# Down projection of a gated FFN in seven block products instead of eight, in five stages instead of three

## What is computed

```python
def conv_ffn(hn, w_ffn_in, conv_w, conv_b, w_ffn_down):
    dt = hn.dtype
    u, v = jnp.split(hn @ w_ffn_in, 2, axis=-1)
    pad = CONV_W // 2
    up = jnp.pad(u, ((0, 0), (pad, pad), (0, 0)))
    L = u.shape[1]
    uc = conv_b
    for t in range(CONV_W):
        uc = uc + up[:, t:t + L] * conv_w[t]
    return (jax.nn.gelu(uc) * v).astype(dt) @ w_ffn_down
...
        h = h + conv_ffn(rmsnorm(h, norm_ffn[l]), w_ffn_in[l], conv_w[l], conv_b[l],
                         w_ffn_down[l])
    return rmsnorm(h, norm_final)
```

## Time and profile before

| | us |
|---|---|
| median of 3 runs | 1263.61 |
| the profiled execution | 1264.54 |
| its span | 1262.7 |
| FFN from the last long stop of PE to the end (769.58 to 1262.70) | 493.1 |
| of it: up projection | 305.4 |
| down chunks 1 and 2 | 66.1 each |
| last chunk with the end | 55.5 |

### The profile page before, as it was taken

The page is one execution under the profiler, slowest core; times in us unless marked ns, Lnnn a source line. Parts: engine busy times, 40 slices in busy tenths (PEclk is TensorE's granted clock), DMA queues, the critical chain, the costliest instruction groups (busy, mean ns, idle before and its releaser), DMA issues.

```text
span 1262.7 us, 18036 instructions
## 1 busy us (share of the span) xinstructions
PE 1232.3 (98%) x7088; PEld 1120.7 (89%) x7088; DVE 711.9 (56%) x969; ACT 490.9 (39%) x724; POOL 128.9 (10%) x93
## 2 busy tenths in 40 slices
PE   6999999999999999999999988999999999999998
PEld 5999899989998998888888878998889998899986
DVE  7494586377368463223223698775237774337755
ACT  5353344245146152212221255554125653135534
POOL 0000000000000000000000303430124420124200
PEclk9999999999999999999999999999999999999999
DMA  4311111101121112121215102222201213112122
GB/s 171 136 35 51 63 51 51 62 33 50 34 78 36 46 37 68 67 67 50 76 56 184 34 34 86 82 68 78 89 34 67 67 42 121 72 34 81 53 84 100
DMA packets 23180, 86.10 MB, mean 68 GB/s; under 512 B 2512, under 2 KB 2768, under 8 KB 23120
## 3 DMA queue, kind: packets, MB, share of 16 engines
q1 hardware_dynamic: 22544, 83.90, 19.4%
q10 hardware_dynamic: 576, 1.38, 0.3%
HBM read 82.12 MB, written 3.15 MB: 68 GB/s over the span
## 4 chain that ended last, share of the span: by engine, by line
PE 92%; DVE 4%; DMA 1%; issue 1%; ACT 1%; DVEq 1%; SPq 0%; ACTq 0%
PE ps L1425 58%; PE ps L1669 23%; PE ps L1522 3%; PE ps L1462 3%; PE ps L1515 1%; PE ps L1532 1%; PE ps L1450 1%; DVE af L1196 1%; PE ps L1452 1%; DVE h L1137 1%; DMA raw<-in_units 1%; DVE ring L1150 1%; PE ps L1407 0%; PE ps L1498 0%; PE ps L1507 0%
## 5 line engine op out<-in xcount | busy, mean ns | idle before, releaser
L1425 PE MATMUL ps<-hn,ring 128*128 128x256 f32 (+1 forms) x2544 | 462.5, 337 | 0.3 <-DVE hn L839 0.3
L1425 PEld LDWEIGHTS ps<-hn,ring 128*128 128x128 f32 x2544 | 388.3, 191 | 46.7 <-issue 0.7
L1669 PE MATMUL ps<-af,ring 128*128 128x384 f32 x1848 | 325.7, 336 | 10.9 <-DVE af L1196 3.9
L1669 PEld LDWEIGHTS ps<-af,ring 128*128 128x128 f32 x1848 | 321.3, 189 | 15.0 <-DVE af L1196 4.8
L1425 PE MATMUL ps<-ring,g 128*128 128x512 f32 x792 | 180.9, 390 | 0.8 <-issue 0.8
L1425 PEld LDWEIGHTS ps<-ring,g 128*128 128x128 f32 x792 | 148.4, 188 | 32.6 <-issue 2.0
L810 DVE TENSOR_TENSOR ring<-raw,ring 128x1024 fp32r<-128x1024 f32 x68 | 83.1, 1224 | 119.2 <-ACT ring L415 114.8
L464 ACT ACTIVATE sig<-ps 128x768 f32<-128x768 f32 x36 | 29.2, 812 | 179.9 <-PE ps L1425 179.8
L1150 DVE TENSOR_TENSOR ring<-raw,ring 128x512 fp32r<-128x512 f32 x88 | 74.0, 877 | 15.9 <-ACT ring L652 15.7
L415 ACT ACTIVATE ring<-raw 128x1024 fp32r<-128x1024 f32 x68 | 71.7, 1055 | 28.8 <-PE ps L1425 10.2
L1384 POOL TENSOR_TENSOR sums<-raw 128x512 f32<-128x512 f32 x1 | 1.3, 1289 | 706.9 <-DMA raw<-in_pairs 706.9
(11 more groups left out here) (158 smaller groups left out, 1210.5 us busy)
## 6 DMA issues: line engine op xcount, KB each, us to landing
raw<-in_units SPq DMA_DIRECT2D x90, 512.0 KB, 3.5
raw<-in_pairs SPq DMA_DIRECT2D x44, 512.0 KB, 3.4
strips<-in_strips SPq DMA_DIRECT2D x4, 896.0 KB, 4.5
x_in<-in_x_s SPq DMA_DIRECT2D x4, 512.0 KB, 5.5
h<-in_x_s SPq DMA_DIRECT2D x1, 2048.0 KB, 8.4
y_s<-hw SPq DMA_DIRECT2D x4, 512.0 KB, 2.6
x_in<-in_x_p SPq DMA_DIRECT2D x2, 512.0 KB, 7.5
h<-in_x_p SPq DMA_DIRECT2D x1, 1024.0 KB, 10.5
```

The costliest lines, as they stand in the source:

```text
L1425: ins = pe.matmul(out, w if stationary_w else x, x if stationary_w else w, start=start and i == 0, stop=stop and i == 2)
L1669: ins = pe.matmul(ps[:, bank, 0:HALF], ring[:, p, a, k * P:(k + 1) * P], af[:, x, b, k, :], start=first and k == 0 and j == 0, stop=k == H ...
```

## The change

w_ffn_down is made in seven block products too. A down pair q is gate tiles 2q and 2q+1 (11 pairs) by both halves of the output. The 2x2 blocks are: the tokens in two halves of 384 by the two gate tiles, and the two gate tiles by the two halves of the output. One product of a pair is 3 token tiles by 3 passes = 9 matmuls of 512 columns, so a pair is 63 matmuls (before: 2 gate tiles by 6 token tiles by 2 halves by 3 passes = 72).

- Stages: up pairs 0 to 4, then down pairs 0 and 1; 5 to 8, then 2 and 3; 9 to 12, then 4 and 5; 13 to 16, then 6 and 7; 17 to 21, then 8, 9 and 10. So all but the last stage take gate tiles that were made at least one up pair ago.
- Weight side: down pairs are loaded into the same two raw buffers in turn with the up pairs. They get the same four differences on POOL and 7 pieces of 512 columns through the ring. The difference S1 is now made in place over A11, so it waits until A11 is split. Pair 10 has a third buffer over `af`.
- Gate side: `gate` of an even tile writes `ge`. `gate` of an odd tile writes `cb` and makes four sums (S3, S2, S1, S4) of 384 columns. Seven forms are split into `gf`: one behind the even tile and six behind the odd tile. Before, one 768-column split followed each tile.
- Results: each of the 7 products of a stage ends in 3 residual sums of 128x512 on DVE (21 per stage, 105 in all; before 36). The next but one product writes the same banks and waits for them.
- End: the last product (A22) is made token tile by token tile for tiles 3 to 5, 9 matmuls each; tiles 0 to 2 are finished behind the product S4. Before, all six were finished one by one, behind 18 matmuls each.

The core of the diff:

```diff
-CHUNKS = ((0, 8), (8, 16), (16, 22))
+STAGES = ((0, 5, (0, 1)), (5, 9, (2, 3)), (9, 13, (4, 5)), (13, 17, (6, 7)), (17, 22, (8, 9, 10)))
+DOWN = [(A11, A12, S2, S1, S3, S4, A22)] * 4 + [(A11, A12, S2, S1, S4, S3, A22)]
+DEST = {A11: (0, 0), A12: (0, 0), S2: (0, 1), S1: (1, 1), S3: (1, 1), S4: (0, 1), A22: (1, 0)}
+ON_A = (A11, S2, S3, A22)
+        def difference(eng, j, x):
+            if x == S1:
+                eng.wait_ge(pu_ld[raw_of(j)], 16 * loads_of(j))
+                eng.wait_ge(pv_ld[raw_of(j)], 16 * loads_of(j))
+                eng.wait_ge(flo, ORD[j, A11] + 1)
+                ins = eng.tensor_tensor(b11, b12, b11, ALU.subtract)
+            elif x == S2:
...
+                ins = eng.tensor_tensor(second, b22, b11, ALU.subtract)
+        def down_bank(hi, x, t):
+            return 2 + t if x in ON_A else (5, BANK_A[hi % 2], 1)[t]
...
+            for j in SEQ:
+                b, prior = raw_of(j), prior_of(j)
...
                     sp.wait_ge(flo, ORD[prior, A22] + 1)
+                sp.dma_start(raws[b][:, 0, :], pairs[j, 0]).then_inc(pu_ld[b], 16)
                 if prior is not None:
                     sp.wait_ge(flo, ORD[prior, S4] + 1)
+                sp.dma_start(raws[b][:, 1, :], pairs[j, 1]).then_inc(pv_ld[b], 16)
...
             def gate(i):
+                q = i // 2
...
+                if i % 2 == 0:
+                    dve.tensor_tensor(ge[:], cb[:], v2[:], ALU.mult).then_inc(g32_done, 1)
+                    return
                 dve.tensor_tensor(cb[:], cb[:], v2[:], ALU.mult).then_inc(g32_done, 1)
+                dve.tensor_tensor(GATE[S3], ge[:, 0:HALF], ge[:, HALF:T], ALU.subtract).then_inc(gs_done, 1)
+                dve.tensor_tensor(GATE[S2], GATE[A22], GATE[S3], ALU.subtract).then_inc(gs_done, 1)
+                dve.tensor_tensor(GATE[S1], ge[:, HALF:T], GATE[A22], ALU.add).then_inc(gs_done, 1)
+                if i == NF - 1:
+                    gate_lo(i - 1)
+                dve.tensor_tensor(GATE[S4], GATE[A12], GATE[S2], ALU.subtract).then_inc(gs_done, 1)
...
+                for n, x in enumerate(DOWN[d]):
+                    if hi < NF or n < 6:
+                        lo_upto(PLACE[down_pair(qs[-1]), x] + 5)
+                    if hi < NF:
+                        down_sums(d, hi, qs, x, range(3))
+                        if n == 0:
+                            gate(hi - 1)
+                        elif n == 1:
+                            gate_lo(hi - 1)
+                        continue
...
+                    elif x == S3:
+                        dve.drain()
+                        for t in range(3, NT):
+                            dve.tensor_tensor(hw[:, t, early(t)], h[:, t, early(t)], wfin[:, early(t)], ALU.mult).then_inc(weighed, 1)
...
+            def down(hi, qs, d):
+                for n, x in enumerate(order):
+                    last = d == len(STAGES) - 1 and n == 6
+                    steps = [(q, t) for t in range(3) for q in qs] if last else [(q, t) for q in qs for t in range(3)]
+                    for q, t in steps:
                         if t == 0:
+                            pe.wait_ge(flo, ORD[down_pair(q), x] + 1)
+                            pe.wait_ge(g_lo, gate_form(q, x))
+                        if q == q0:
...
+                            elif x in (S2, S1, S3, S4, A22):
+                                before = {S2: A11, S1: A12, S3: S2, S4: S1, A22: S3}[x]
+                                pe.wait_ge(h_up, base + 3 * order.index(before) + t + 1)
```

More of the change, by code:

```diff
@@ new lines, in _ @@
+            base, order = down_base(len(STAGES) - 1), DOWN[-1]
+            for t in range(3):
+                act.wait_ge(h_up, base + 3 * order.index(S4) + t + 1)
+                squares(t, late(t), stat[:, 0, t:t + 1]).then_inc(sq_done, 1)
+            act.wait_ge(var_done, 2 * NT + 1)
+            act.activation(stat[:, 2, 0:3], stat[:, 1, 0:3], ACT.Sqrt).then_inc(sd_done, 1)
+            act.wait_ge(root_done, 1)
+            act.wait_ge(weighed, 3)
+            for t in range(3):
+                act.activation(hw[:, t, early(t)], hw[:, t, early(t)], ACT.Copy, scale=stat[:, 3, t:t + 1]).then_inc(out_rdy0, 1)
@@ L1309, in _ @@
                         join_third(i)
[L1310 to L1311 removed]
+                    if i > lo and i < NF - 1:
+                        gate_lo(i - 1)
                 lo_upto(PLACE[hi - 1, A22] + 5)
@@ L1329, in _ @@
-            dve.wait_ge(fin_ld, 16)
-            dve.wait_ge(fdone, len(ORD))
-            dve.drain()
-            for t in range(NT):
-                dve.tensor_tensor(hw[:, t, 0:PIECE], h[:, t, 0:PIECE], wfin[:, 0:PIECE], ALU.mult).then_inc(weighed, 1)
-            dve.wait_ge(half_sq, NT)
-            dve.tensor_scalar(stat[:, 5, :], stat[:, 4, :], 1.0 / D, EPS, ALU.mult, ALU.add).then_inc(half_var, 1)
-            for t in range(NT):
-                dve.wait_ge(dn, (2 * len(CHUNKS) - 1) * NT + t + 1)
-                residual(t, 1, t)
+                if hi == NF:
+                    gate(NF - 1)
+                    gate_lo(NF - 1)
@@ L1393, in _ @@
                 combine_tokens(pool, 0, x, s_done, 0)
-            combine(1, A22)
-            for i in range(2, NF):
-                for x in (S1, S3, S2, A22):
-                    combine(i, x)
+            pool.wait_ge(t_done, DIFF[1, S3])
+            for j, x in DIFFS[7:]:
+                difference(pool, j, x)
         @blk.tensor
@@ L1784, in _tables @@
+            for d, (lo, hi, qs) in enumerate(STAGES):
+                ffn(lo, hi, d)
+                down(hi, qs, d)
 def _tables():
@@ L1821, in _units @@
     out += [rows(w_out, k, half) for half in range(2) for k in range(KD // 2)]
-    for f0, f1 in CHUNKS:
-        out += [rows(w_ffn_down, k, half) for half in range(2) for k in range(f0 // 2, f1 // 2)]
     assert len(out) == UNITS
     pairs = [np.stack([cols(w_ffn_in, f * P), cols(w_ffn_in, FF + f * P)]) for f in range(NF)]
+    pairs += [np.stack([rows(w_ffn_down, q, 0), rows(w_ffn_down, q, 1)]) for q in range(NQ)]
     return np.stack(out), np.stack(pairs)
```

411 lines of the change are left out of this document (196 added, 215 removed).

## The result

The changed kernel takes 1284.28 us (median of 4 runs, 1282.7 to 1285.21), beside 1263.6 for the kernel before (4 runs, 1263.3 to 1263.95). The ratio is 1.0162, with a 95% interval of 1.0145 to 1.018. The profiled execution took 1282.7 us, its span is 1280.9. Forecast were 1253.2 us and a range of 1245 to 1264: the sign was wrong, and the time lies outside the range.

The account below looks back on a forecast made before the run. PE was taken as the bound, 98% busy, so time is matmuls times a rate. Up stages 307.0, down stages 118.9 and last stage 56.8 sum to 482.7 against 493.1: 10.4 us less, 1253.2 for the median, range 1245 to 1264.

Parts of the forecast that it names:

- five up stages: Up products of the FFN: 305.4 us before, plus 1.6 for stops at two more stage ends, so 307.0.
- four down stages: The first four down stages, two down pairs each: 29.7 us per stage including 1.0 loss, 118.9 in all.
- last stage and end: From the last down stage's start to the span's end: 55.9 us against 55.5 before, 56.8 with the clock.
- Matmuls: Down projection: 693 matmuls for 792, 99 fewer at 0.228 us each, 22.6 us less, all on PE's path.
- Down stages: DVE late through each down stage, S4's sums delaying the next up stage: 1.0 us loss each, ends 0 and 2.5.
- DVE in an up pair: DVE needs 10.8 us behind even tiles, 15.3 behind odd, mean 13.1 of PE's 14.6: hidden, nothing taken.
- sharp point: Next up pair's S1 needs `join_last` 10.4 us after S3 ended; ready at 8.8 to 10.2, so nothing taken.
- rival 3: Clock falls at each down stage's stop: four times 1.8 us, 1260.4; no change by this or half of rival 2: 0.10.
- Last stage: PE stands 2.7 us in the last down stage, waiting for the late gate tile's form for A11 of pair 10.
- The clock's 0.9: Lower clock behind the last stage's gate stop, 1.8 us in the earlier trace, may or may not follow: 0.9 taken.
- The end's count of DVE's instructions: DVE's work behind the last products: last stage and end 55.9 us against 55.5, so 6.2 of the gain lost.
- Rival 2: DVE bounds the down stages at S4's sums; all splits doubled, 5.6 us per stage, 1275.6. Slower: chance 0.15.

Follow-up runs that it names:

- experiment 1: Changed kernel with POOL's differences of the down pairs made over 8 of 512 columns, output not the reference's: 1249.67 us.
- experiment 2: Changed kernel with the four gate sums of each odd tile made over 8 of 384 columns, output not the reference's: 1271.42 us.
- experiment 3: Changed kernel with each 512-column POOL difference made as two instructions of 256 columns: 1285.3 us.
- experiment 4: Changed kernel with POOL holding a stage's down-pair differences until DVE made the third join of the last up pair: 1291.06 us.
- experiment 5: Changed kernel with the four gate sums of an odd tile behind the third join on DVE instead of ahead: 1285.95 us.
- experiment 6: Changed kernel; DVE makes down differences S1 and S2 (last stage: first pair only), POOL's S3 and A22 wait for residual sums; some DVE work reordered: 1262.98 us.
- experiment 7: As experiment 6, but DVE makes all eight down differences in each of the first four stages, POOL none: 1269.8 us.
- experiment 8: As experiment 6, with weight splits ahead of S3, S4, A22 reaching one piece less far, and DVE making all last-stage S1 and S2: 1253.71 us.
- experiment 9: As experiment 8, with last-stage A11 and A12 of pair 10 after those of pairs 8 and 9, weight splits two pieces less far there: 1249.45 us.

## Why the prediction was wrong, by its steps

Forecast were 482.7 us from the start of the FFN. Measured are 512.2, from 768.68 us on, 0.9 earlier than before: 29.5 more in the FFN, 28.6 more in the profiled time (1282.7 for 1254.1). By the terms:

| term | forecast | after | experiment 1 |
|---|---|---|---|
| five up stages | 307.0 | 335.8 | 308.9 |
| four down stages | 118.9 | 115.2 | 115.1 |
| last stage and end | 56.8 | 61.2 | 55.1 |
| sum | 482.7 | 512.2 | 479.1 |

(The down stages are 4 x 28.8, the last row is from the start of the last stage's first down matmul to the end of the span, and the up stages are the rest.)

- *Matmuls.* Right: 99 fewer, the rest at 0.228 us.
- *Down stages.* Forecast a loss of 1.0 each, came none. The splits average 0.84 to 0.86 us in them, within the 0.79 to 0.89 of the working, and a residual costs 0.63 instead of 0.68, 1.0 us less for the 21 of a stage. The differences of the next up pair start 22.2 us into the stage (947.27), where some 23 was forecast.
- *DVE in an up pair.* This step failed. It named the "sharp point" as `join_last` ahead of the next S1 and took nothing for it; for the last pair of a stage it said that the six splits of the odd tile end at -0.2 and that `join_third` is about 1.3 us late. Two things were wrong in it. First, it priced the odd tile's sums at 2.1 us and its product at the time alone, with POOL counted only in the mean of the weight splits (0.79), as if the differences stayed spread out. The row of 910.47 shows POOL released by one weight split, and from there nothing holds it: six differences run together, just where the sums are. Second, it had no line for who waits behind the sums. PE is ready for S4 2.9 us after S3 ended (0.58 and 2.35), and goes on 0.6 us behind the start of the third join (920.66, 921.25), so the join must start by 2.3. Without the burst it starts 1.3 after S3, as forecast (907.26 in experiment 1, where S3 ended at 905.95): a reserve of 1.0 us. The burst adds 9.84 - 3.56 = 6.3 us, 1.05 per difference, which is the reserve and the stop of 5.2. Four stops make 21.0 us.
- *The clock, rival 3.* Forecast for these stages: none. Behind the stop the 12 matmuls of the last product take 3.98 us, where half of the 24 in experiment 1 takes 2.23: 1.8 us each. (The four stages together last 375.7 us in after and 346.4 in experiment 1; less the stops of 21.0 that leaves 8.3, or 2.1 each.) The price of the rival (1.8 from the earlier trace rows) was right, its place not: the stop that does it is another one. Stops and clock together are 29.3 us. Less 2.4 in the last up stage, where experiment 1 stood 0.7 us longer and lost 1.6 to a lower clock (24 matmuls in 6.02 us for 4.43), and plus the 1.9 by which experiment 1 lies above 307.0, they are the 28.8 of the first row.
- *Last stage.* The gate's stop was forecast as 2.7 and is 2.83 in experiment 1, 6.82 in after, by the burst's 4.0 us on the convolution. The clock's 0.9 is 2.3 (35.10 for 32.8); in experiment 1 it is 0.1. The end's count of DVE's instructions holds: 55.1 against 55.9 without the clock term.
- *Rival 2* had the right resource ("now three differences run in a burst") and the wrong place and price. It priced DVE per weight split, doubled at most, at the S4 sums of the down stages. What decides is the number of POOL instructions that run while DVE has only instructions of that kind, each adding about 1.05 us, and it falls on the short sums as hard as on the long splits. The rival's worst case was 1275.6; the measured time lies above it.

The row that should have warned is the two splits of 2.38 us in the earlier trace rows: 0.5 us over their own 0.68 each, beside a single difference of 1.58. I read it as a ratio near 1.75 and averaged it over seven splits. Read as 1.0 us per difference, six differences add 6 us ahead of a join that has a reserve of about 1.0.

Some smaller figures of the working don't come out of its own terms, without changing its outcome. Of DVE's three waits in the earlier trace rows one (1.33) is for ACT, not for PE. The end loses 6.6 us of the gain, not 6.2 (55.9 against 55.5 less 27 x 0.228). With free stages and full clock the sum is 1248.2, not 1247.8. And the bounds of the terms give 1248.3 to 1264.1, not 1246 to 1261.

What stays open: why the down stages lost nothing was read from the means alone, the stops that the burst leaves behind the residuals in experiments 2 and 3 were not split into price and order, and no run looked at a down stage of three pairs with full clock ahead of it.

## What to carry to other kernels

Price contention per instruction of the other engine, not as a factor on your own: count how many of its instructions fall between two points that someone waits for, and multiply. Look for bursts: an engine whose inputs are all there works them off in a row when one release comes, and a mean taken over a stage hides it. If the colliding work must be done, put it beside instructions that don't collide (here the residuals), and hold it there by a wait, rather than shift the engine's own queue: experiments 4 and 5 only moved the stop, 6 to 9 removed it.

## What the runs showed of the hardware

**DVE and POOL take turns by whole instructions.** In the rows of after, POOL's first difference runs to 912.05. The product (0.95 us in experiment 1) started at 910.82, is recorded with 2.05 and ends at 912.87: 0.95 behind 911.9, so it began about when POOL ended. POOL's next starts at 912.13 and lasts 1.86, which is the 1.29 of experiment 6 plus 0.57, about to where the product ends (spans on POOL are rough; DVE's carry the argument). So an instruction's recorded time is its wait and its own time:

| DVE instruction, two operands in SBUF | alone | beside a 512-column difference |
|---|---|---|
| 8 columns | 0.16 | 1.23, 1.15 |
| 384 columns | 0.55 | 1.47 to 1.62 |
| 512 columns | 0.68 | 1.75 |
| 768 columns | 0.95 | 2.05 |
| 384 columns, difference of 256 | 0.55 | 1.09 |
| residual of 512, one operand in PSUM (mean of three in a row) | 0.63 | 0.63 |

The added time is 0.9 to 1.1 us in the first four rows, whatever the instruction's size. The turns are not strict: in experiment 5 POOL's first difference is recorded with 3.04 us from 911.76, while DVE's product (0.95) and split (0.69) beside it keep their own times, so there POOL waited for more than one instruction of DVE. The Trainium skill states this kind of rule (SBUF — State Buffer, section "SBUF: two separate sides"): the port pair that the two engines share is an exclusive lock that a VectorE instruction with two SBUF inputs, or the GpSimd instruction, holds for its whole length, while the other blocks. The recorded times agree, the untouched residual among them. In this kernel the price is what is left of a running difference, 0.9 to 1.1 us.

**A stop's length alone doesn't tell whether the clock falls.** Busy time by stretch in after (us, PE, PEld, DVE, ACT, POOL; then the granted clock):
```profile
826.15:829.80 3.65, 3.65 (x13) 3.65 (x14) 3.65 (x8) 0.78 (x2) 0.00 (x0) 0.58 0.02 4
...
1230.70:1235.00 4.30, 4.25 (x10) 3.40 (x11) 4.29 (x9) 2.65 (x6) 0.00 (x0) 0.50 0.01 4
```
Behind 5.2 us of stop the clock is 0.58 over the next 3.65 us, behind 6.82 us it is 0.50, the lower level (1.2 GHz), for 4.3. Experiment 1 kept full clock behind its stop of 2.83 us (the first row), but in the same run shows 0.72 behind one of 2.25 us (the second):
```profile
1200.00:1202.00 2.00, 2.00 (x9) 1.65 (x10) 2.00 (x5) 1.51 (x4) 0.00 (x0) 1.00 0.03 8
...
1187.00:1193.00 6.00, 6.00 (x25) 6.00 (x26) 1.76 (x3) 2.60 (x5) 1.77 (x5) 0.72 0.00 0
```
Experiment 8 kept it behind 3.3 us and fell to 0.57 behind 4.0:
```profile
1190.00:1194.00 4.00, 4.00 (x23) 4.00 (x24) 3.93 (x7) 2.06 (x5) 0.00 (x0) 1.00 0.00 0
1202.50:1206.00 3.50, 3.49 (x9) 2.83 (x10) 3.50 (x8) 2.61 (x6) 0.00 (x0) 0.57 0.03 7
```
What else decides was not tried. The Trainium skill's rule on short frequent pauses between groups that cycle through PSUM banks (TensorE: Matmul & The Clock Gate, "A second HAM failure mode: psum-queue depth-cycling") did not bite: the down stages change bank with every third matmul and run at 0.228 us per matmul without a fall, even behind the slow product. The rows of after show no pause within a down stage, so they test the rule only in part. Experiment 7 does pause there (0.92 and 1.25 us within the first down stage), with a granted clock of 1.00 from 822.7 to 855: pauses that short and that few left it alone.
